# A mixer stage in another order: weight units, head statistics, convolution taps, roundings, low parts and a norm on TensorE, ScalarE and VectorE

## The chip, the cores and the metric

The kernel is one program on one core of a Trainium2 chip. The core has TensorE (PE, matmuls; PEld is its weight load), VectorE (DVE), ScalarE (ACT), GpSimd (POOL) and SyncE (SP), which here does nothing but issue DMAs. The metric is the device time of one execution in microseconds, lower is better; a kernel is judged by the median of its runs.

## The reference

Two transformer-like blocks of two layers each run on 256 tokens of 1024 channels in fp32. Every layer has a swiglu part, a mixer part and a swiglu part. The change touches the mixer of the first block, which runs twice (layer 0 and layer 1). Cut to its core:

```python
hn = _modulate(_rms_norm(h, norm_g[l, 1]), sh2, sc2)
z = hn @ w_in[l]                                   # 2564 columns
qa, ka = rms_norm per 32 channels of z             # dq, dk
o_a = differential_attention(qa, ka, va, lam)      # dv is the value
o_b = silu(layer_norm(conv31(a * sigmoid(g)) + b)) # ca, cg
u, v = split(gelu(z[..., GMLP0:FOX_Q0]))           # gu, gv
o_c = u * (W_s @ layer_norm(v) + bias)
log_f = log_sigmoid(z[..., FOX_F0:IN_COLS] + fb)   # f: four columns
o_d = forgetting_attention(rms_norm(q), rms_norm(k), v, log_f)   # fq, fk, fv
h = h + g2 * (concat(o_a, o_b, o_c, o_d) @ w_out[l])
```

`mod = silu(c) @ ada_w[l] + ada_b[l]` gives the shifts, scales and gates. Its 1024 x 3072 slice for the NEXT part is computed inside the present part, on VectorE.

## The kernel before

**Weight units.** All weights pass in units of 128x2048 fp32 (1 MB), unit k in slot k mod 3 of three buffers. SP loads a unit into `raw` (L375), ScalarE rounds it to fp32r, `whi` (`hi(L, k)`, L1117), VectorE subtracts that from it, `wlo` (`lo(L, k)`, L1648), and TensorE makes each product in three matmuls (L533 to L535), so that it needs `lo` of the unit and therefore `hi` and the load. In the mixer, units 0 to 10 are slices of `w_in` in the order fv, dv, gv, f, dq, dk, ca, cg, fq, fk, gu, and units 11 to 14 are `w_out`. I write z5 for TensorE's work on unit 5. f has four columns and is small. ScalarE copies the result of each unit out of PSUM (`copy(i)`, L1441); two PSUM banks take turns.

**Modulation tiles.** VectorE also multiplies 24 tiles of `ada_w` (128x1024, 0.5 MB each, L1775), `ada(m, q)`, written `tiles(first, last)`. There are two tile buffers.

**SP's queue.** SP is one queue in order. In the mixer it issues, for i = 0, 1, 2 ...: load of unit i, then tiles 2i-6 and 2i-5. Each has a wait of its own in that queue:

```python
sp.wait_ge(lo_done, L.unit(k, i) + 1)          # load: lo of unit k-3 is done
sp.wait_ge(adam_used, 24 * (m - 1) + q + 1)    # tile q: ada(q-2) is done
```

So the queue's order there is: load 6, tiles 6 and 7, load 7, tiles 8 and 9, load 8, tiles 10 and 11, load 9, and so on. Since tile 7 waits for ada(5), load 7 stands behind a wait for ada(5); load 8 behind one for ada(7), load 9 behind one for ada(9).

**The rest around the change.** On TensorE: `head_stat` (L784, mean squares of heads; the first needs the Square of dq and dk, L1468), `gmix` (L1026, needs the gmlp norm `gv`, L2133), `diff_scores` (L748), `taps` (L994, one 31-tap convolution diagonal each, from six buffers that POOL fills, L2294), `turn` (L767). On ScalarE: `rs` (L1283, L1284: Ln, then Exp, for 1/root), the forget gate's Abs, Exp and Ln (L1459 to L1461, each waits for VectorE's `fx`), softmax (L1295). On VectorE: the gelu and layer norm of gv (L2092 to L2133), the cumulative sum of the forget gates (L2142 to L2147, needs `fl` of ScalarE), `head_norm` (L1656 to L1659, L2099, needs `rs`), `conv_in` (L2166), `logits` (L1864 to L1879). Every engine goes through its own list in order and stops at the first wait that isn't met.

Of the kernel before, what the change touches and what calls it, by code (L numbers as in the profile page):

```python
# [5 lines left out]
ALU = mybir.AluOpType  # L6
# [34 lines left out]
def program(nc, x, c, ada_w, ada_b, norm_g, ffn1_w_in, ffn1_w_out, ffn2_w_in, ffn2_w_out, w_in, w_out,  # L41
# [5 lines left out]
    S = x.shape[1]  # L47
# [11 lines left out]
    with ExitStack() as ctx:  # L59
# [469 lines left out]
        def _(pe):  # L529
# [439 lines left out]
            def mix0(L, n, j, k0):  # L969
                l, m, at = L.l, n + 1, k0 + len(ZU1)  # L970

                def z(i):
                    unit_z(L, n, k0, i, ZU1[i][2])
# [4 lines left out]
                def diff_scores(c):  # L978
                    dq, dk = halves("dq"), halves("dk")
                    if c == 0:  # L980
                        pe.wait_ge(s["diffqk"], l + 1)
                    else:
                        pe.wait_ge(s["scores_read"], seq(L, ROUNDS, 1))
                    scores(L, st, dq, lambda r, w, ch: dk[r:r + w, ch, :],
                           lambda h: (64 * (h % 2) + 32 * c, h // 2), 32)
# [31 lines left out]
                z(3)  # L1017
                z(4)
                z(5)

                pe.wait_ge(s["gv"], l + 1)
                v = zt["gv"].rearrange("p (b e) -> p b e", b=2)
# [5 lines left out]
                ins.then_inc(s["gmix"], 1)  # L1028

                head_stat(L, 0, 0, blk32, sq8, [ps[:, 6, :], ps[:, 7, :]])  # L1030
                z(6)
                z(7)
                diff_scores(0)
                z(8)
                diff_scores(1)
                taps(0, 8)
                z(9)
                head_stat(L, 1, 1, blk64, sq8, [ps[:, 6, :], ps[:, 7, :]])
                taps(8, 16)
                z(10)  # L1040
                turn(L, 0, S0)
                taps(16, 24)
# [46 lines left out]
        def _(act):  # L1089
# [344 lines left out]
            def mix0(L, n, j, k0):  # L1434
                l, m = L.l, n + 1

                def copy(i, func=ACT.Copy):

                    used(L, k0 + i)
                    w = S if ZU1[i][2] == "F" else 2 * S  # L1440
                    act.activation(Z[:, i, 0:w], ps[:, i % 2, 0:w], func).then_inc(z_copied[0], 1)  # L1441

                hi(L, k0 + 2)
                copy(0)
                hi(L, k0 + 3)
                copy(1)
                hi(L, k0 + 4)
                copy(2)

                copied(L, zi["gv"])  # L1450
                act.activation(zt["cg"], zt["gv"], ACT.Square).then_inc(s["gu_sq"], 1)
                act.wait_ge(s["gu_t"], 2 * l + 1)
                act.activation(zt["cg"], zt["cg"], ACT.Sigmoid, scale=-GELU_B).then_inc(s["gu_e"], 1)

                hi(L, k0 + 5)
                copy(3)
                act.wait_ge(s["fx"], l + 1)
                f, w = zt["f"][0:4, 0:S], zt["f"][0:4, S:2 * S]
                st(act.activation(w, f, ACT.Abs))  # L1459
                st(act.activation(w, w, ACT.Exp, scale=-1.0))  # L1460
                act.activation(w, w, ACT.Ln, bias=ones_col[0:4, 0:1]).then_inc(s["fl"], 1)  # L1461

                hi(L, k0 + 6)
                copy(4)
                hi(L, k0 + 7)
                copy(5)
                copied(L, zi["dk"])
                act.activation(sq8h[0], Z[:, zi["dq"]:zi["dq"] + 2, :].rearrange("p a n -> p (a n)"),  # L1468
                               ACT.Square).then_inc(s["sq"], 1)
                rs(st, L.event(0), sq8h[1], stat2)  # L1470
                hi(L, k0 + 8)
                copy(6)
                hi(L, k0 + 9)
                act.wait_ge(s["gv"], l + 1)
                copy(7, ACT.Sigmoid)
                hi(L, k0 + 10)
                copy(8)
                softmax(L, 0, S0)
                hi(L, k0 + 11)
                copy(9)  # L1480
                copied(L, zi["fk"])
                act.activation(sq8h[0], Z[:, zi["fq"]:zi["fq"] + 2, :].rearrange("p a n -> p (a n)"),
                               ACT.Square).then_inc(s["sq"], 1)
                softmax(L, 1, S1)
                act.wait_ge(s["conv_in"], l + 1)
                rs(st, L.event(1), zca, stat2)
                hi(L, k0 + 12)
                copy(10)

                copied(L, zi["gu"])  # L1490
                act.wait_ge(s["scores"], seq(L, ROUNDS, 2))
                act.activation(zt["dq"], zt["gu"], ACT.Square).then_inc(s["gu_sq"], 1)
                turned_out(L, 0, PT1)
                act.wait_ge(s["gu_t"], 2 * l + 2)
                act.activation(zt["dq"], zt["dq"], ACT.Sigmoid, scale=-GELU_B).then_inc(s["gu_e"], 1)
                act.wait_ge(s["gu"], l + 1)
                act.activation(xo(4, 6), zt["gu"], ACT.Copy).then_inc(s["outh"], 1)

                act.wait_ge(s["pv"], seq(L, TURNS, 1))
                act.wait_ge(s["foxqk"], l + 1)  # L1500
                act.activation(u8[:, 1536:2048], ps[:, 7, :], ACT.Square).then_inc(s["sq"], 1)
                rs(st, L.event(2), sq8[:, 1536:2048], ps[:, 6, :])
                softmax(L, 2, S1)
                act.wait_ge(s["dout"], l + 1)
                act.activation(xo(0, 2), s0f[:, 1024:1536], ACT.Copy).then_inc(s["outh"], 1)

                act.wait_ge(diag_used, TAPS * (l + 1))
                for ch in range(2):
                    act.activation(zt["ca"][:, ch * S:ch * S + S], ps[:, PVB, ch * S:ch * S + S], ACT.Identity,
                                   bias=prm[:, CB + 2 * l + ch:CB + 2 * l + ch + 1]).then_inc(s["conv_done"], 1)  # L1510
                hi(L, k0 + 13)
                turned_out(L, 1, PT1)
                act.wait_ge(s["craw"], l + 1)
                act.activation(zt["cg"], zt["ca"], ACT.Square, scale=2.0).then_inc(s["sq"], 1)
                rs(st, L.event(3), nrm[:, 0, :], ps[:, 0, S:2 * S])
                act.wait_ge(s["pv"], seq(L, TURNS, 2))
                act.activation(xo(6, 8), ps[:, PVB, :], ACT.Copy).then_inc(s["outh"], 1)
                summed(m, 0)
                hi(L, k0 + 14)
                summed(m, 1)  # L1520
                act.wait_ge(s["cy"], 2 * l + 1)
                act.activation(zt["cg"], zt["ca"], ACT.Sigmoid).then_inc(s["cexp"], 1)
                act.wait_ge(s["cy"], 2 * l + 2)
                act.activation(xo(2, 4), zt["ca"], ACT.Copy).then_inc(s["outh"], 1)
                hi(L, k0 + 15)
                summed(m, 4)
                summed(m, 5)
# [12 lines left out]
        def _(dve):  # L1540
# [540 lines left out]
            def mix0(L, n, j, k0):  # L2081
# [26 lines left out]

                v = zt["gv"].rearrange("p (b e) -> p b e", b=2)
                gelu_in(1, zt["gv"], zt["cg"])  # L2110
                tiles(4, 5)
                dve.wait_ge(s["gu_e"], 2 * l + 1)
                st(tt(zt["gv"], zt["gv"], zt["cg"], ALU.mult))
                for b in range(2):
                    ins = dve.bn_stats(lnst[:, b, :], v[:, b, :])
                st(ins)
                dve.sem_inc(dve_waited, 1)
                for b in range(2):
                    ins = dve.bn_aggr(lnmv[:, b, :], lnst[:, b, :])
# [5 lines left out]
                for _ in range(3):  # L2125
                    st(tt(tmp, y, y, ALU.mult))
                    st(tt(tmp, tmp, half, ALU.mult))
                    st(stt(y, tmp, 1.5, y, ALU.add, ALU.mult))
                for b in range(2):
                    ins = ts(v[:, b, :], v[:, b, :], lnmv[:, b, 0:1], y[:, b:b + 1], ALU.subtract, ALU.mult)  # L2130
                st(ins)
                st(tt(v, v, ngb[:, 0, l:l + 1, :].to_broadcast([P, 2, 256]), ALU.mult))
                tt(v, v, ngb[:, 1, l:l + 1, :].to_broadcast([P, 2, 256]), ALU.add).then_inc(s["gv"], 1)  # L2133
                tiles(5, 6)
                lo(L, k0 + 5)

                copied(L, zi["f"])
                f, w = zt["f"][0:4, 0:S], zt["f"][0:4, S:2 * S]
                ts(f, f, fb[0:4, l:l + 1], None, ALU.add).then_inc(s["fx"], 1)
                tiles(6, 8)  # L2140
                dve.wait_ge(s["fl"], l + 1)
                st(stt(f, f, 0.0, w, ALU.min, ALU.subtract))  # L2142
                dve.tensor_tensor_scan(gcum[0:4, 0, 0:P], ones_row[0:4, :], f[:, 0:P], 0.0, ALU.mult, ALU.add)
# [1 line left out]
                st(dve.tensor_tensor_scan(gcum[0:4, 0, P:S], ones_row[0:4, :], f[:, P:S], gcum[0:4, 0, P - 1:P],  # L2145
                                          ALU.mult, ALU.add))
                ts(gcum[0:4, 1, :], gcum[0:4, 0, :], -1.0, None, ALU.mult).then_inc(s["foxcum"], 1)  # L2147
                lo(L, k0 + 6)
                tiles(8, 10)
                lo(L, k0 + 7)  # L2150

                dve.wait_ge(s["gmix"], l + 1)
                tg = zt["gv"].rearrange("p (c b t) -> p c b t", c=2, b=2)
# [1 line left out]
                for b in range(2):  # L2155
                    ins = tt(tg[:, :, b, :], mg[:, :, b, :], bsb[:, l, :, :], ALU.add)
                ins.then_inc(s["gmixed"], 1)
                tiles(10, 12)
                head_norm(0, sq8h[1], diffg, ("dq", "dk"), "diffqk")
                lo(L, k0 + 8)  # L2160
                tiles(12, 14)
                lo(L, k0 + 9)

                copied(L, zi["cg"])
                dve.memset(ypad[:, :, 0:CONVK - 1], 0.0)
                tt(ypad[:, :, CONVK - 1:], ca2, zt["cg"].rearrange("p (c t) -> p c t", c=2),  # L2166
                   ALU.mult).then_inc(s["conv_in"], 1)

                logits(L, st, 0, S0, amask, 32 ** -0.5)
                tiles(14, 16)  # L2170
                lo(L, k0 + 10)
# [171 lines left out]
```

## Time and profile before

| | |
|---|---|
| median of 3 runs (lowest, highest) | 2483.33 us (2475.29, 2487.5) |
| the profiled execution's own time | 2485.93 us |
| its span | 2484.1 us |
| PE, PEld, DVE, ACT busy | 92%, 77%, 65%, 45% |
| mean granted TensorE clock | 0.97 |
| DMA | 452.76 MB, 182 GB/s in the mean |

The span is that of all instructions; the time is 1.8 us more. A 92% busy PE bounds the kernel, and what can be won or lost is PE's idle time (and stretches at half clock). The first block's mixer runs from about 265 to 450 us (layer 0) and again from about 860 to 1045 us (layer 1).

### The profile page before, as it was taken

What the parts mean: (1) busy time and instruction counts of PE and PEld (TensorE: products, weight loads), DVE (VectorE), ACT (ScalarE), POOL (GpSimd) and SP (SyncE); (2) the same over time, 40 slices, a digit from 0 to 9 for tenths busy, and PEclk for the clock granted to TensorE, in tenths of its full rate; (3) what the DMA queues carried; (4) which work ended last, traced back from release to release, by engine and by line L of the source; (5) the groups of instructions that cost most, each with busy time, mean ns of one, the idle gap of its engine ahead of it and who ended that gap; (6) DMA issues with size and microseconds to landing.
All of it is one profiled execution on the core that took longest, in us unless ns stands there. A gap on an engine that the chain in (4) does not pass through costs nothing.

```text
span 2484.1 us, 31758 instructions
## 1 busy us (share of the span) xinstructions
PE 2297.6 (92%) x11778; PEld 1922.9 (77%) x11788; DVE 1604.2 (65%) x1886; ACT 1115.4 (45%) x1304; POOL 120.0 (5%) x176
## 2 busy tenths in 40 slices
PE   1999899899899989899989999989999998998998
PEld 0787777688688777678878889977877888997887
DVE  6686794676677677555565568675555556856555
ACT  1443463444444455344444456644444446564443
POOL 1000023000000004200000000000000000000000
PEclk9999998999999998899999999999999999999999
DMA  7787552587488564255555554345555555434653
GB/s 251 254 309 237 171 199 85 175 285 258 131 295 282 164 214 142 94 169 187 185 169 186 188 151 136 119 151 188 186 169 171 185 186 144 144 102 136 198 184 108
DMA packets 321123, 452.76 MB, mean 182 GB/s; under 512 B 32406, under 2 KB 269832, under 8 KB 320008
## 3 DMA queue, kind: packets, MB, share of 16 engines
q1 hardware_dynamic: 314160, 439.43, 54.1%
q0 software_dynamic: 2816, 9.51, 1.2%
q10 hardware_dynamic: 4056, 2.58, 0.4%
q8 instruction: 60, 0.98, 0.2%
q14 instruction: 31, 0.25, 0.0%
HBM read 450.43 MB, written 1.05 MB: 182 GB/s over the span
## 4 chain that ended last, share of the span: by engine, by line
PE 76%; DVE 13%; ACT 4%; issue 2%; POOL 1%; DMA 1%; ACTq 1%; DVEq 0%; SPq 0%
PE ps L540 18%; PE ps L541 18%; PE ps L542 18%; PE ps L533 3%; DVE wlo L1648 3%; PE ps L534 3%; PE ps L535 3%; PE ps L994 2%; PE ps L639 1%; POOL side L2294 1%; ACT whi L1117 1%; DMA arena<-in_ada_w_dram 1%; PE ps L748 1%; DVE arena L1775 1%; PE ps L589 1%
## 5 line engine op out<-in xcount | busy, mean ns | idle before, releaser
L1648 DVE TENSOR_TENSOR wlo<-raw,whi 128x2048 fp32r<-128x2048 f32 (+1 forms) x348 | 791.7, 2278 | 472.1 <-ACT whi L1117 472.1
L1117 ACT ACTIVATE whi<-raw 128x2048 fp32r<-128x2048 f32 x346 | 659.8, 1909 | 271.9 <-PE ps L542 235.6
L540 PE MATMUL ps<-whi,xl 128*128 128x512 f32 x1472 | 597.8, 406 | 22.9 <-DVE u L1792 22.9
L541 PE MATMUL ps<-wlo,xh 128*128 128x512 f32 x1472 | 579.1, 393 | 0.0
L542 PE MATMUL ps<-whi,xh 128*128 128x512 f32 x1472 | 578.4, 393 | 0.0
L540 PEld LDWEIGHTS ps<-whi,xl 128*128 128x128 f32 x1472 | 279.6, 190 | 86.4 <-DVE u L1792 26.3
L542 PEld LDWEIGHTS ps<-whi,xh 128*128 128x128 f32 x1472 | 279.6, 190 | 61.1
L541 PEld LDWEIGHTS ps<-wlo,xh 128*128 128x128 f32 x1472 | 279.8, 190 | 59.7 <-issue 4.8
L533 PE MATMUL ps<-xl,whi 128*128 128x256 f32 x864 | 254.0, 294 | 23.0 <-DVE wlo L1648 23.0
L540 PE MATMUL ps<-whi,hidl 128*128 128x512 f32 x640 | 252.2, 394 | 0.0
L542 PE MATMUL ps<-whi,hidh 128*128 128x512 f32 x640 | 249.2, 389 | 0.0
L541 PE MATMUL ps<-wlo,hidh 128*128 128x512 f32 x640 | 249.1, 389 | 0.0
L534 PE MATMUL ps<-xh,wlo 128*128 128x256 f32 x864 | 248.2, 287 | 0.0
L535 PE MATMUL ps<-xh,whi 128*128 128x256 f32 x864 | 247.9, 287 | 0.0
L1233 ACT ACTIVATE hidh<-ps 128x512 fp32r<-128x512 f32 x80 | 47.9, 599 | 319.6 <-PE ps L639 319.6
L533 PEld LDWEIGHTS ps<-xl,whi 128*128 128x128 f32 x864 | 169.8, 196 | 27.3 <-DVE wlo L1648 21.7
L534 PEld LDWEIGHTS ps<-xh,wlo 128*128 128x128 f32 x864 | 170.0, 197 | 1.1 <-issue 1.0
L535 PEld LDWEIGHTS ps<-xh,whi 128*128 128x128 f32 x864 | 169.6, 196 | 0.0
L1775 DVE SCALAR_TENSOR_TENSOR arena<-arena,condT 128x1024 f32<-128x1024 f32 x120 | 154.4, 1286 | 19.5 <-DMA arena<-in_ada_w_dram 17.8
L1229 ACT ACTIVATE sq<-ps 128x256 f32<-128x256 f32 x176 | 67.5, 384 | 219.4 <-PE ps L542 218.9
L1796 DVE TENSOR_TENSOR hidl<-ps,hidh 128x512 fp32r<-128x512 f32 x80 | 55.4, 692 | 160.6 <-ACT hidh L1233 160.6
L540 PEld LDWEIGHTS ps<-whi,hidl 128*128 128x128 f32 x640 | 120.2, 188 | 25.9 <-issue 1.4
(367 smaller groups left out, 2612.6 us busy)
## 6 DMA issues: line engine op xcount, KB each, us to landing
raw<-in_ffn_w_in_dram SPq DMA_DIRECT2D x176, 512.0 KB
arena<-in_ada_w_dram SPq DMA_DIRECT2D x128, 512.0 KB, 5.8
raw<-in_w_in_dram SPq DMA_DIRECT2D x54, 1024.0 KB
raw<-in_ffn_w_out_dram SPq DMA_DIRECT2D x44, 1024.0 KB
raw<-in_w_ffn_gate_dram SPq DMA_DIRECT2D x88, 512.0 KB
raw<-in_w_ffn_up_dram SPq DMA_DIRECT2D x88, 512.0 KB
raw<-in_w_ffn_down_dram SPq DMA_DIRECT2D x44, 1024.0 KB
raw<-in_w_out_dram SPq DMA_DIRECT2D x16, 1024.0 KB
```

Of the source, the lines that this page charges most:

```text
L533: pe.matmul(o, wh, al, start=start, stop=False, **kw)
L534: pe.matmul(o, wl, ah, start=False, stop=False, **kw)
L535: return pe.matmul(o, wh, ah, start=False, stop=stop, **kw)
L540: pe.matmul(o, al, wh, start=start, stop=False, **kw)
L541: pe.matmul(o, ah, wl, start=False, stop=False, **kw)
L542: return pe.matmul(o, ah, wh, start=False, stop=stop, **kw)
L994: pe.matmul(ps[:, PVB, ch * S:ch * S + S], diag[d % RING], ypad[:, ch, tap:tap + S], start=(tap == 0), stop=(tap == CONVK - 1)).then_inc(d ...
L1117: act.activation(whi[:, k % 3, :], raw[:, k % 3, :], ACT.Copy).then_inc(hi_done, 1)
L1229: act.activation(sig[:, a, :], ps[:, a, 0:256], ACT.Sigmoid).then_inc(sig_ready, 1)
L1648: tt(a[0], a[1], a[2].bitcast(F32), ALU.subtract).then_inc(lo_done, 1)
L1775: stt(seg, adam[:, at, :], scalar, seg, ALU.mult, ALU.add).then_inc(adam_used, 1)
L1796: tt(hidl[:, :, :].rearrange("p f t -> p (f t)"), ps[:, HT, :], hidh[:, :, :].bitcast(F32).rearrange("p f t -> p (f t)"), ALU.subtract).th ...
```

## The change

Only the order in which TensorE, ScalarE and VectorE go through their lists in `mix0` is changed, in the first third of it; SP's and POOL's lists stay as they are. On TensorE z6 moves ahead of `gmix`, z8 ahead of the first `diff_scores`, the first eight taps between the two `diff_scores`, and taps 8 to 16 ahead of the second `head_stat`. On ScalarE `hi` of units 5, 6 and 7 moves ahead of the forget gate's functions, and `rs` behind `hi` of units 8 and 9. On VectorE `lo` of units 5 to 9 moves earlier and the tiles later.

```diff
 # TensorE
+                z(6)
                 pe.wait_ge(s["gv"], l + 1)
...
                 head_stat(L, 0, 0, blk32, sq8, [ps[:, 6, :], ps[:, 7, :]])
-                z(6)
                 z(7)
+                z(8)
                 diff_scores(0)
-                z(8)
+                taps(0, 8)
                 diff_scores(1)
-                taps(0, 8)
                 z(9)
+                taps(8, 16)
                 head_stat(L, 1, 1, blk64, sq8, [ps[:, 6, :], ps[:, 7, :]])
-                taps(8, 16)
                 z(10)
 # ScalarE
                 act.activation(zt["cg"], zt["gv"], ACT.Square).then_inc(s["gu_sq"], 1)
+                hi(L, k0 + 5)
                 act.wait_ge(s["gu_t"], 2 * l + 1)
                 act.activation(zt["cg"], zt["cg"], ACT.Sigmoid, scale=-GELU_B).then_inc(s["gu_e"], 1)
-                hi(L, k0 + 5)
                 copy(3)
+                hi(L, k0 + 6)
+                copy(4)
+                hi(L, k0 + 7)
                 act.wait_ge(s["fx"], l + 1)
...
-                hi(L, k0 + 6)
-                copy(4)
-                hi(L, k0 + 7)
                 copy(5)
...
-                rs(st, L.event(0), sq8h[1], stat2)
                 hi(L, k0 + 8)
                 copy(6)
                 hi(L, k0 + 9)
+                rs(st, L.event(0), sq8h[1], stat2)
 # VectorE
                 gelu_in(1, zt["gv"], zt["cg"])
-                tiles(4, 5)
+                lo(L, k0 + 5)
...
+                copied(L, zi["f"])
+                ts(f, f, fb[0:4, l:l + 1], None, ALU.add).then_inc(s["fx"], 1)
...
+                lo(L, k0 + 6)
                 for b in range(2):
                     ins = ts(v[:, b, :], v[:, b, :], lnmv[:, b, 0:1], y[:, b:b + 1], ALU.subtract, ALU.mult)
...
-                tiles(5, 6)
-                lo(L, k0 + 5)
-                copied(L, zi["f"])
-                ts(f, f, fb[0:4, l:l + 1], None, ALU.add).then_inc(s["fx"], 1)
-                tiles(6, 8)
+                tiles(4, 6)
+                lo(L, k0 + 7)
                 dve.wait_ge(s["fl"], l + 1)
...
-                lo(L, k0 + 6)
-                tiles(8, 10)
-                lo(L, k0 + 7)
+                tiles(6, 8)
                 dve.wait_ge(s["gmix"], l + 1)
...
+                lo(L, k0 + 8)
+                tiles(8, 10)
+                lo(L, k0 + 9)
+                head_norm(0, sq8h[1], diffg, ("dq", "dk"), "diffqk")
                 tiles(10, 12)
-                head_norm(0, sq8h[1], diffg, ("dq", "dk"), "diffqk")
-                lo(L, k0 + 8)
-                tiles(12, 14)
-                lo(L, k0 + 9)
...
+                tiles(12, 14)
                 logits(L, st, 0, S0, amask, 32 ** -0.5)
```

VectorE's list before, in layer 0, from `lo` of unit 5 on. L1648 is a `lo`, here of units 5, 6 and 7; L1775 is a modulation tile, here 6 and 7, 8 and 9, then 10 and 11.

```order
 L1648 TENSOR_TENSOR wlo<-raw,whi 128x2048
 L2139 TENSOR_SCALAR arena<-arena,fb 4x256
 L1775 SCALAR_TENSOR_TENSOR arena<-arena,condT 128x1024 x2
 L2142 SCALAR_TENSOR_TENSOR arena<-arena 4x256
 L2143 SCALAR_TENSOR_TENSOR arena<-ones_row,arena 4x128
 L2145 SCALAR_TENSOR_TENSOR arena<-ones_row,arena 4x128
 L2147 TENSOR_SCALAR arena<-arena 4x256
 L1648 TENSOR_TENSOR wlo<-raw,whi 128x2048
 L1775 SCALAR_TENSOR_TENSOR arena<-arena,condT 128x1024 x2
 L1648 TENSOR_TENSOR wlo<-raw,whi 128x2048
 L2156 TENSOR_TENSOR arena<-ps,side 128x2x128 x2
 L1775 SCALAR_TENSOR_TENSOR arena<-arena,condT 128x1024 x2
```

The changed kernel's list, from the tiles 4 and 5 on. The L1648 rows are `lo` of units 7, 8 and 9, and the L1775 rows tiles 4 and 5, 6 and 7, 8 and 9.

```order
 L1775 SCALAR_TENSOR_TENSOR arena<-arena,condT 128x1024 x2
 L1648 TENSOR_TENSOR wlo<-raw,whi 128x2048
 L2141 SCALAR_TENSOR_TENSOR arena<-arena 4x256
 L2142 SCALAR_TENSOR_TENSOR arena<-ones_row,arena 4x128
 L2144 SCALAR_TENSOR_TENSOR arena<-ones_row,arena 4x128
 L2146 TENSOR_SCALAR arena<-arena 4x256
 L1775 SCALAR_TENSOR_TENSOR arena<-arena,condT 128x1024 x2
 L2153 TENSOR_TENSOR arena<-ps,side 128x2x128 x2
 L1648 TENSOR_TENSOR wlo<-raw,whi 128x2048
 L1775 SCALAR_TENSOR_TENSOR arena<-arena,condT 128x1024 x2
 L1648 TENSOR_TENSOR wlo<-raw,whi 128x2048
 L1656 TENSOR_TENSOR u<-sq 128x1024
```

Before, `lo` of unit 7 stood behind tile 9; now it stands directly behind tile 5, that of unit 8 behind tile 7, and that of unit 9 directly behind tile 9.

ScalarE's list, changed kernel, in the same place, with the semaphores that each waits for. L1117 are `hi` of units 5, 6, 7 and then 8 and 9; L1462 to L1464 are the forget gate's functions (L1459 to L1461 before).

```order
 L1117 ACTIVATE whi<-raw 128x2048 [waits unit_used,raw_loaded1]
 L1462 ACTIVATE arena<-arena 4x256 [waits fx]
 L1463 ACT_TABLE_LOAD
 L1463 ACTIVATE arena<-arena 4x256 [waits act_step]
 L1464 ACT_TABLE_LOAD
 L1464 ACTIVATE arena<-arena,ones_col 4x256 [waits act_step]
 L1441 ACTIVATE arena<-ps 128x512 [waits unit_used]
 L1468 ACTIVATE sq<-arena 128x1024 [waits z_copied0]
 L1117 ACTIVATE whi<-raw 128x2048 [waits unit_used,raw_loaded2]
 L1441 ACTIVATE arena<-ps 128x512 [waits unit_used]
 L1117 ACTIVATE whi<-raw 128x2048 [waits unit_used,raw_loaded0]
 L1283 ACTIVATE sq<-ps,epsc 128x1024 [waits ms_ready]
```

The first row is `hi` of unit 7, which was behind the forget gate's functions and now stands ahead of them, of `copy(5)` and of the Square (L1468); the last is `rs`, which was ahead of `hi` of unit 8 and now stands behind `hi` of unit 9.

## Rows read from the trace of the kernel before

**Rows 1.** TensorE's waits, 260 to 420 us: total, times, longest

```profile
PE ps L533 <- DVE wlo L1648: 7.0, 2, 6.1
PE ps L994 <- POOL side L2294: 5.0, 7, 1.4
...
PE ps L784 <- ACT sq L1482: 1.8, 1, 1.8
```

**Rows 2.** Windows: length, busy PE, PEld, DVE, ACT, POOL; PEclk, DMA share, GB/s

```profile
293.00:300.00 7.00, 6.02 (x48) 5.82 (x48) 6.35 (x20) 2.71 (x3) 0.00 (x0) 1.00 0.95 326
...
306.00:308.00 2.00, 1.97 (x9) 1.97 (x10) 1.90 (x3) 1.71 (x3) 0.00 (x0) 0.50 1.02 376
```

**Rows 3.** Timeline of TensorE: start, us, instruction, idle before and releaser

```profile
306.03 0.58 PE L533 MATMUL ps<-xl,whi 128*128 128x256 f32 x1 [6.06 <-DVE wlo L1648]
...
313.69 1.15 PE L1026 MATMUL ps<-arena 128*64 128x128 f32 x16
315.93 1.98 PE L784 MATMUL ps<-sq,blk 128*128 128x512 f32 x4 [1.09 <-ACT sq L1468]
317.35 0.68 PE L533 MATMUL ps<-xl,whi 128*128 128x256 f32 x1
...
346.76 0.47 PE L533 MATMUL ps<-xl,whi 128*128 128x256 f32 x1
...
365.65 1.47 PE L767 MATMUL ps<-ident,arena 128*128 128x128 f32 x12
```

**Rows 4.** SP's DMA issues in order of time (tiles L450, unit loads L375)

```profile
296.43 7.76 SPq L450 DMA_DIRECT2D arena<-in_ada_w_dram  x2
304.30 0.41 SPq L375 DMA_DIRECT2D raw<-in_w_in_dram  x1
...
317.47 0.41 SPq L375 DMA_DIRECT2D raw<-in_w_in_dram  x1
```

**Rows 5.** Timeline of VectorE

```profile
296.26 0.68 DVE L2113 TENSOR_TENSOR arena<-arena 128x512 f32<-128x512 f32 x1
...
302.50 1.28 DVE L1775 SCALAR_TENSOR_TENSOR arena<-arena,condT 128x1024 f32<-128x1024 f32 x1
...
310.26 0.41 DVE L2142 SCALAR_TENSOR_TENSOR arena<-arena 4x256 f32<-4x256 f32 x1 [1.45 <-ACT arena L1461]
...
312.06 2.29 DVE L1648 TENSOR_TENSOR wlo<-raw,whi 128x2048 fp32r<-128x2048 f32 x1
314.27 2.67 DVE L1775 SCALAR_TENSOR_TENSOR arena<-arena,condT 128x1024 f32<-128x1024 f32 x2
...
322.03 1.29 DVE L1775 SCALAR_TENSOR_TENSOR arena<-arena,condT 128x1024 f32<-128x1024 f32 x1 [1.03 <-DMA arena<-in_ada_w_dram]
323.23 1.22 DVE L1656 TENSOR_TENSOR u<-sq 128x1024 f32<-128x1024 f32 x1
...
329.07 2.28 DVE L1648 TENSOR_TENSOR wlo<-raw,whi 128x2048 fp32r<-128x2048 f32 x1
...
340.46 2.69 DVE L1775 SCALAR_TENSOR_TENSOR arena<-arena,condT 128x1024 f32<-128x1024 f32 x2
...
360.53 1.76 DVE L2184 TENSOR_TENSOR arena<-arena,u 128x1536 f32<-128x1536 f32 x1
```

**Rows 6.** Timeline of ScalarE

```profile
306.26 0.42 ACT L1459 ACTIVATE arena<-arena 4x256 f32<-4x256 f32 x1 [8.56 <-DVE arena L2139]
...
317.95 1.12 ACT L1283 ACTIVATE sq<-ps,epsc 128x1024 f32<-128x1024 f32 x1 [2.07 <-PE ps L784]
...
321.35 1.90 ACT L1117 ACTIVATE whi<-raw 128x2048 fp32r<-128x2048 f32 x1
...
325.27 1.92 ACT L1117 ACTIVATE whi<-raw 128x2048 fp32r<-128x2048 f32 x1 [0.97 <-DMA raw<-in_w_in_dram]
```

**Rows 7.** Layer 1: TensorE's longest wait; tiles 8 and 9; `hi` of unit 9

```profile
PE ps L533 <- DVE wlo L1648: 5.9, 1, 5.9
...
911.08 2.67 DVE L1775 SCALAR_TENSOR_TENSOR arena<-arena,condT 128x1024 f32<-128x1024 f32 x2
...
922.36 1.92 ACT L1117 ACTIVATE whi<-raw 128x2048 fp32r<-128x2048 f32 x1 [1.25 <-DMA raw<-in_w_in_dram]
```

More of the change, by code:

```diff
@@ L2116, in mix0 @@
                 st(ins)
+                copied(L, zi["f"])
+                f, w = zt["f"][0:4, 0:S], zt["f"][0:4, S:2 * S]
+                ts(f, f, fb[0:4, l:l + 1], None, ALU.add).then_inc(s["fx"], 1)
                 dve.sem_inc(dve_waited, 1)
@@ L2133, in mix0 @@
                 tt(v, v, ngb[:, 1, l:l + 1, :].to_broadcast([P, 2, 256]), ALU.add).then_inc(s["gv"], 1)
-                tiles(5, 6)
-                lo(L, k0 + 5)
-                copied(L, zi["f"])
-                f, w = zt["f"][0:4, 0:S], zt["f"][0:4, S:2 * S]
-                ts(f, f, fb[0:4, l:l + 1], None, ALU.add).then_inc(s["fx"], 1)
-                tiles(6, 8)
+                tiles(4, 6)
+                lo(L, k0 + 7)
                 dve.wait_ge(s["fl"], l + 1)
```

## The prediction

> **What bounds the kernel now.** I read the busy shares first, then TensorE's waits, its timeline, and those of the engines that feed it. TensorE is busy 92% of the span, so only its idle time and its slow stretches count. In the mixer of layer 0 its longest wait is for the low part of a weight unit: 7.0 us in two waits, of which the larger, 6.06, stands ahead of z5 [rows 1, 3]; layer 1 has the same, 5.9 us [rows 7]. The reader is to see what VectorE does meanwhile: from 296.26 on it goes through the norm of gv, then through tile 5 at 302.50 [rows 5], and only behind that comes `lo` of unit 5. After the gap the granted clock is at half, 0.50 [rows 2]: z5 took 313.69 - 306.03 = 7.66 us [rows 3], where the 48 matmuls of a unit at full clock take 6.02 [rows 2], so 1.64 more are lost. These 7.7 us a layer are what the new order can aim at. Otherwise TensorE waits there 1.09 us for the first head statistics [rows 3], 1.8 for the second, and 5.0 in all for POOL's diagonals [rows 1].
>
> **What else hangs on that order.** SP's list. Tiles 6 and 7 hold SP from 296.43 to 304.19, and load 7 goes out at 304.30 [rows 4]: half a microsecond after VectorE ended tile 5, at 302.50 + 1.28 = 303.78 [rows 5]. Load 9 goes out at 317.47 [rows 4], again half a microsecond after tile 9 ended, at 314.27 + 2.67 = 316.94 [rows 5]. What holds a load is the tile ahead of it in the queue, since `lo` of three units back was done long before. The trip from "tile 9 done on VectorE" to "unit 9 in SBUF" (the start of its `hi`, which waited for DMA) took 325.27 - 316.94 = 8.3 us [rows 5, 6], and in layer 1, from 913.75 to 922.36, 8.6 [rows 7]. It brings 2.1 MB, two tiles and a unit. Before, it is hidden: between tile 9 and `lo` of unit 9 VectorE has four more tiles, a head norm and two other `lo`.
>
> The Trainium skill (DMA: Bandwidth & Descriptors, "Anatomy of one DMA — SWDGE (gpsimd) path") says that a semaphore wait of a DMA is spent on the issuing sequencer, ahead of dispatch, and that the DMA engines only work off their queues. That speaks against this change, and the trace agrees with it.
>
> **The change, step by step** (layer 0, on the clock of before; a trip is taken as R = 8.0 us, a little under the two rows, because behind both a further tile was in the queue).
>
> Gain. z5 starts where z4 ends, 293.95 + 6.02 = 300.0, at full clock, with z6 right behind it until 312.0; before, z6 ended at 317.35 + 6.02 = 323.4 [rows 3]. TensorE is 11.4 us ahead, and `gmix` (1.15) ends at 313.2. The low parts are in time for it: `hi` of unit 5 can end at about 296, `lo` takes 2.2, so 298; of the norm (302.50 - 296.26 = 6.2 in all) some 4.1 stand ahead of `lo` of unit 6, and the bias of the gate 0.3, so it ends at 304.7.
>
> First trip. The last 2.1 of the norm and tiles 4 and 5 (2.6) bring VectorE to 309.4; it ended tile 5 at 303.78 before. Only then tile 7 and load 7 are issued, and unit 7 is there at 317.4. ScalarE has stood at `hi` of unit 7 since 302, and behind it in its list are the functions of the gate, the copy of z5 and the Square for the first `head_stat`. `hi` 1.9 gives 319.3, the functions 310.26 - 306.26 = 4.0 [rows 5, 6], copy 0.5, Square 1.1: 324.9. TensorE waits for that from 313.2, 11.7 us. Then `head_stat` 317.35 - 315.93 = 1.4 and a restart at half clock, 1.6: 327.9, and z7 until 333.9.
>
> Second trip. VectorE has `lo` of unit 7 by 321.6, waits for the gate until 323.3, cumulative sum 312.06 - 310.26 = 1.8 [rows 5], tiles 6 and 7 2.6: 327.7. Trip 335.7, `hi` 337.6, `lo` 339.8. TensorE waits 5.9 us; z8 with 1.6 of slow clock until 347.4.
>
> Third trip. Tiles 8 and 9 end at 342.4, trip 350.4, `hi` of unit 9 352.3. Only now comes `rs`: 321.35 - 317.95 = 3.4 [rows 6], 355.7, and `head_norm` 329.07 - 323.23 = 5.8 [rows 5], 361.5. The first `diff_scores` waits for it: 14.1 us of idle TensorE, then 3.2 and 1.6 of slow clock, 366.3, and eight taps, 5.1. VectorE does tiles 10 and 11 and `conv_in` until 364.8. Tile 13 is issued at 364.1 and lands some 5.1 later, as tile 11 did (issued after 316.94, used at 322.03 after a wait for DMA) [rows 5]; done at 370.5, the reading half of `logits` 1.9, 372.4. The second `diff_scores` runs until 375.6, where z9 starts; before it started at 346.76 [rows 3]: 28.8 us later.
>
> Given back. The 1.8 us wait at the second `head_stat` goes, since the taps cover it: 27.0. But `turn` waits for both softmaxes. Before, they took from 340.5 to 362.3, 21.8 [rows 5], of which ScalarE was held some 3 by the copy of z9, which isn't so now: from 374.3 to 393.1, against 365.65 [rows 3], 27.5 later. Behind that all follows as before; loads 10 and 11 are issued by 370 and are no limit.
>
> Sum: + 27.5 us a layer, two layers, + 55. The profiled execution took 2485.93, so 2540.9; the median of the runs is 2.6 under it, and I say 2538. The two moves of taps have no price of their own: POOL fills the same six buffers either way.
>
> **Bounds.** R at most 8.6 [rows 7], + 1.8 a layer. At least: 2.1 MB at 376 GB/s [rows 2] is 5.6 us, and the first tile of a pair leaves 1.3 us ahead of R's start, so 4.3 with nothing for start and completion, - 11 a layer. A restart costs 1.6 in the one case seen; after longer gaps 0 to 3 at each of three, - 5 to + 4 a layer.
>
> The Trainium skill's fit for one DMA (same page and section: about 2.0 us plus bytes at 436 GB/s) gives 6.8 us for 2.1 MB as an estimate, 5.5 from R's start; the sum by it would be 2523. This kernel's rows say 8.3 and 8.6, and I keep to them.
>
> **Rivals.**
> (a) Forecast: three exposed trips of 6.5 to 8.6 us with the work in series behind them, + 19 to + 33 a layer, 2521 to 2549. Chance 0.80.
> (b) Short trips: while VectorE stands still nothing follows in the queue, and a trip costs 5.6, the pure transfer at 376 GB/s; 3 x 2.4 = 7 less a layer, and with little lost clock 3 less again: + 17, 2517. Against it: tile 11 alone took 5.1. Chance 0.09.
> (c) Longer: the clock stays at half over much of 313 to 366 us, where TensorE works under half of the time; + 5 to 8 a layer more, 2548 to 2554. Chance 0.06.
> (d) Faster, the other side: SP doesn't hold load 7 behind tile 7. Then the early `lo` gains the 7.7 us and the 1.1 at the first `head_stat` a layer and nothing is given back, 2466. It decides if load 7 leaves before about 300. Against it: SP sat 7.76 us at tiles 6 and 7 with load 7 next in its list [rows 4]. Chance 0.03.
> (e) No change: the stalls are taken out of later waits. In the whole mixer TensorE waits little else than the 5.0 and 1.8 us of [rows 1]. Chance 0.02.
>
> Even trips of 0 us would not make it faster: 27.5 - 24 leaves 3.5 a layer, since `hi`, the functions of the gate, the Square, `rs` and `head_norm` now stand in series.
>
> **Numbers.** The likeliest is (a), 2538. The range takes in (a), most of (b) and (c): 2516 to 2556. A change within 0.5% (12 us) can't be told from none. Slower 0.95, within 0.02, faster 0.03.
>
> **What would show it.** Right: z5 and z6 run without a gap from 294 to 312; SP issues load 7 near 310, load 8 near 328, load 9 near 343, each half a microsecond behind the end of a tile; `hi` of units 7, 8 and 9 each wait for DMA; TensorE has gaps of about 12, 6 and 14 us ahead of the first L784, of z8 and of the first `diff_scores`; z9 starts near 376; the same again in layer 1. Wrong: load 7 issued before 305, or gaps that close because a trip takes under 5 us.

## The result, and the profile after

| | before | changed kernel |
|---|---|---|
| median of the runs | 2480.65 us (4 runs) | 2539.16 us (4 runs, 2535.13 to 2539.61) |
| span of the profiled execution | 2484.1 us | 2537.8 us |
| mean granted TensorE clock | 0.97 | 0.96 |

The ratio is 1.0231, 95% interval 1.0215 to 1.0248: 2.3% slower. Forecast were 2538 us and a range of 2516 to 2556. The span grew by 53.7 us. Three single executions, one each of the kernel before (5455 us), of experiment 1 (4585) and of experiment 2 (5814), lie far outside all others and are left out of the medians and ratios below.

TensorE's waits in the changed kernel, first layer 0, then layer 1. Each row has the total in us, how often, and the longest:

```profile
PE ps L748 <- DVE arena L2099: 14.9, 1, 14.9
PE ps L784 <- ACT sq L1468: 12.5, 1, 12.5
PE ps L533 <- DVE wlo L1648: 6.4, 2, 5.5
...
PE ps L748 <- DVE arena L2099: 14.7, 1, 14.7
PE ps L784 <- ACT sq L1468: 12.7, 1, 12.7
PE ps L533 <- DVE wlo L1648: 8.8, 2, 7.1
```

The 6.06 us ahead of z5 [rows 1, 3] are gone. In their place stand three gaps a layer: ahead of the first `head_stat` (L784), ahead of z8 (L533) and ahead of the first `diff_scores` (L748).

SP's issues of the changed kernel, layer 0: three times a pair of tiles (L450), then a unit load (L375). They answer to [rows 4]:

```profile
307.22 1.73 SPq L450 DMA_DIRECT2D arena<-in_ada_w_dram  x2
309.05 0.41 SPq L375 DMA_DIRECT2D raw<-in_w_in_dram  x1
325.77 1.72 SPq L450 DMA_DIRECT2D arena<-in_ada_w_dram  x2
327.60 0.41 SPq L375 DMA_DIRECT2D raw<-in_w_in_dram  x1
341.20 1.72 SPq L450 DMA_DIRECT2D arena<-in_ada_w_dram  x2
343.03 0.41 SPq L375 DMA_DIRECT2D raw<-in_w_in_dram  x1
```

VectorE, changed kernel, the same stretch: a pair of tiles (L1775), then the wait ahead of `lo` (L1648):

```profile
305.85 2.68 DVE L1775 SCALAR_TENSOR_TENSOR arena<-arena,condT 128x1024 f32<-128x1024 f32 x2
318.86 2.29 DVE L1648 TENSOR_TENSOR wlo<-raw,whi 128x2048 fp32r<-128x2048 f32 x1 [10.33 <-ACT whi L1117]
...
324.42 2.65 DVE L1775 SCALAR_TENSOR_TENSOR arena<-arena,condT 128x1024 f32<-128x1024 f32 x2
...
337.62 2.29 DVE L1648 TENSOR_TENSOR wlo<-raw,whi 128x2048 fp32r<-128x2048 f32 x1 [9.89 <-ACT whi L1117]
339.83 2.67 DVE L1775 SCALAR_TENSOR_TENSOR arena<-arena,condT 128x1024 f32<-128x1024 f32 x2
352.93 2.29 DVE L1648 TENSOR_TENSOR wlo<-raw,whi 128x2048 fp32r<-128x2048 f32 x1 [10.42 <-ACT whi L1117]
```

ScalarE, changed kernel: `hi` of units 7, 8 and 9, each after a wait for DMA:

```profile
316.92 1.91 ACT L1117 ACTIVATE whi<-raw 128x2048 fp32r<-128x2048 f32 x1 [15.74 <-DMA raw<-in_w_in_dram]
...
335.68 1.91 ACT L1117 ACTIVATE whi<-raw 128x2048 fp32r<-128x2048 f32 x1 [11.44 <-DMA raw<-in_w_in_dram]
...
350.98 1.91 ACT L1117 ACTIVATE whi<-raw 128x2048 fp32r<-128x2048 f32 x1 [12.91 <-DMA raw<-in_w_in_dram]
```

Read the three together. Tile 5 ends at 305.85 + 2.68 = 308.53, load 7 leaves half a microsecond later, unit 7 is used at 316.92: a trip of 8.4 us. The second runs from 327.07 to 335.68, 8.6, the third from 342.50 to 350.98, 8.5. Each time VectorE stands 10 us: the trip and `hi`. Layer 1 has the same picture, with trips of 8.7, 9.3 and 8.6 us.

TensorE, changed kernel: the first row answers to L784 of [rows 3]; the next are the scores and the eight taps between them, z9's first matmul, and `turn`:

```profile
324.30 3.78 PE L784 MATMUL ps<-sq,blk 128*128 128x512 f32 x4 [12.53 <-ACT sq L1468]
...
362.28 5.90 PE L748 MATMUL ps<-arena 32*128 32x128 f32 x16 [14.92 <-DVE arena L2099]
368.11 6.54 PE L994 MATMUL ps<-arena,side 128*128 128x256 f32 x16
374.57 3.60 PE L748 MATMUL ps<-arena 32*128 32x128 f32 x16
378.10 0.58 PE L533 MATMUL ps<-xl,whi 128*128 128x256 f32 x1
...
397.51 1.47 PE L767 MATMUL ps<-ident,arena 128*128 128x128 f32 x12
```

This trace runs 0.8 us ahead of that of before at z4, so `turn` is 397.51 - 365.65 + 0.8 = 32.7 us late [rows 3], and some 6 us of that are given back later in the layer.

### The profile page after: what moved, and what is told of

Read it like the earlier page. It is cut to its first block, busy times and chain, and to the rows that moved or that the text cites. A ratio compares the mean times of both kernels' runs of the same rounds, so it can differ in the third digit from the quotient of the medians.

```text
span 2537.8 us, 31772 instructions
## 1 busy us (share of the span) xinstructions
PE 2303.6 (91%) x11788; PEld 1927.7 (76%) x11788; DVE 1604.1 (63%) x1886; ACT 1114.4 (44%) x1304; POOL 117.1 (5%) x176
## 4 chain that ended last, share of the span: by engine, by line
PE 73%; DVE 14%; ACT 5%; DMA 3%; issue 2%; POOL 1%; ACTq 1%; SPq 0%; DVEq 0%
PE ps L540 18%; PE ps L542 18%; PE ps L541 18%; DVE wlo L1648 3%; PE ps L533 3%; PE ps L534 3%; PE ps L535 3%; DMA raw<-in_w_in_dram 3%; ACT whi L1117 2%; PE ps L639 1%; PE ps L994 1%; DVE arena L1775 1%; PE ps L748 1%; POOL side L2292 1%; PE ps L570 1%
## 5 line engine op out<-in xcount | busy, mean ns | idle before, releaser
L1648 DVE TENSOR_TENSOR wlo<-raw,whi 128x2048 fp32r<-128x2048 f32 (+1 forms) x348 | 791.7, 2278 | 533.6 <-ACT whi L1117 533.6
L1117 ACT ACTIVATE whi<-raw 128x2048 fp32r<-128x2048 f32 x346 | 660.0, 1910 | 393.4 <-PE ps L542 235.6
L533 PE MATMUL ps<-xl,whi 128*128 128x256 f32 x864 | 256.0, 296 | 22.8 <-DVE wlo L1648 22.8
L533 PEld LDWEIGHTS ps<-xl,whi 128*128 128x128 f32 x864 | 171.3, 198 | 28.4 <-DVE wlo L1648 21.5
L1775 DVE SCALAR_TENSOR_TENSOR arena<-arena,condT 128x1024 f32<-128x1024 f32 x120 | 154.2, 1285 | 23.5 <-DMA arena<-in_ada_w_dram 21.7
L541 PEld LDWEIGHTS ps<-wlo,hidh 128*128 128x128 f32 x640 | 120.2, 188 | 26.0 <-issue 1.4
```

The source lines that it names most:

```text
L533: pe.matmul(o, wh, al, start=start, stop=False, **kw)
L541: pe.matmul(o, ah, wl, start=False, stop=False, **kw)
L1117: act.activation(whi[:, k % 3, :], raw[:, k % 3, :], ACT.Copy).then_inc(hi_done, 1)
L1648: tt(a[0], a[1], a[2].bitcast(F32), ALU.subtract).then_inc(lo_done, 1)
L1775: stt(seg, adam[:, at, :], scalar, seg, ALU.mult, ALU.add).then_inc(adam_used, 1)
```

## The experiments

Two accounts were open. **The queue**: what bounds the stretch is a loop, tile on VectorE, SP, DMA, `hi` on ScalarE, `lo` on VectorE, and the change has put VectorE's `lo` directly behind the tiles that free the load. **The engines' own order**: TensorE's z6 and z8 ahead of small work, ScalarE's `hi` ahead of the gate's functions and `rs` behind `hi`, or VectorE's `head_norm` in series with the scores would cost time whatever SP does. Times are medians; "before" ran along each time, 2480.8 us with the first four and 2478.71 with the others. The ratios are to that "before"; the changed kernel has 1.0231 in the same sense.

**1. SP's loads 7 and 8 ahead of tiles 6 and 7** (the changed kernel, SP's list alone edited)

```diff
                                 load(L, k, whole(as8, k, cols8(w_in, l, col)))
-                            tiles(i)
+                            if i < 6:
+                                tiles(i)
+                            elif i > 7:
+                                tiles(i - 2)
...
-                            tiles(11 + g)
+                            tiles(9 + g)
+                        tiles(13)
+                        tiles(14)
```

> The changed kernel with one more edit, in SP's list of the first block's mixer alone: unit loads 7 and 8 go out ahead of tiles 6 and 7, and all later tiles follow two units later in the list (load 9, tiles 8 and 9, load 10, and so on). The engines' lists stay those of the changed kernel. Theory of the queue: what costs is the loop tile on VectorE, SP, DMA, hi, lo; with it cut, load 7 is issued near 293, hi of units 7, 8 and 9 hardly wait for DMA, VectorE's three waits of some 10 us ahead of L1648 go, and about 31 us a layer come back: 2477 us, between 2468 and 2488. Rival, the engines' own order (the functions of the gate behind hi, rs behind hi of unit 9, head_norm ahead of the scores in series): the gaps of TensorE at the first head_stat and the first diff_scores stay for the greater part, over 2510.

Measured 2477.14 us, ratio to before 0.9979 (0.9964 to 0.9994). SP's issues from load 6 on, of this kernel:

```profile
297.18 5.92 SPq L375 DMA_DIRECT2D raw<-in_w_in_dram  x3
312.49 1.75 SPq L450 DMA_DIRECT2D arena<-in_ada_w_dram  x2
```

TensorE's waits in it ahead of the scores (L753), the taps (L999) and `turn` (L772); the lines of this kernel stand 5 further down:

```profile
PE ps L753 <- DVE arena L2104: 4.2, 1, 4.2
PE ps L999 <- POOL side L2297: 2.5, 3, 1.2
PE ps L772 <- DVE arena L2187: 1.8, 1, 1.8
```

Loads 6, 7 and 8 now leave in one stretch from 297.18 (this trace is 5 us late at z4: 298.91 against 293.95), with tiles 6 and 7 behind them. The wait at the first `head_stat` is gone and that at the scores is 4.2 instead of 14.9. With the engines' lists untouched, all 62.0 us (2539.16 to 2477.14) come back. The loss was the loop; with this SP list the engines' order has no loss of its own. Its gain over before is 0.2%, some 2 us a layer. That is much less than the 7.7 us at z5: in this trace the scores and the eight taps behind the 4.2 us wait took 11.7 us at a mean granted clock of 0.56 (335.11 to 346.77). At full clock such scores take 3.2 and eight taps 3.6, so that wait and slow clock together cost about 9 us.

**2. `hi` of unit 7 back behind the Square** (changed kernel, ScalarE)

```diff
                 copy(4)
-                hi(L, k0 + 7)
                 act.wait_ge(s["fx"], l + 1)
...
                                ACT.Square).then_inc(s["sq"], 1)
+                hi(L, k0 + 7)
                 hi(L, k0 + 8)
```

> The changed kernel with hi of unit 7 moved back on ScalarE behind the functions of the forget gate, the copy of z5 and the Square. Theory of the queue: TensorE's 12.5 us wait at the first head_stat goes nearly whole, but the loop through VectorE, SP and DMA stays, so unit 7 lands when it did and a gap of about 7 us opens ahead of z7; VectorE gets the gate's values some 1.6 us earlier; all in all 1.8 us a layer less, 2536 us (2530 to 2540). Rival, TensorE's waits are what counts: 12.5 us a layer less, 2514.

Measured 2533.89 us (median of three; 2532.54 to 2540.51; ratio 1.0221, 1.0199 to 1.0243). TensorE's waits of this kernel, layer 0:

```profile
PE ps L533 <- DVE wlo L1648: 19.6, 3, 9.5
PE ps L748 <- DVE arena L2099: 14.9, 1, 14.9
```

The 12.5 us wait at L784 has vanished and stands again ahead of the weight units, 19.6 us instead of 6.4. The gain over the changed kernel is 5.3 us by the medians and about 2.5 by the ratios, for both layers together and inside the spread of these runs: the 25 us that the rival expected did not come. A wait that an engine shows can be only the place where a loop comes to the surface.

**3. Tiles 4 and 5 ahead of the norm** (changed kernel, VectorE)

```diff
                 lo(L, k0 + 5)
+                tiles(4, 6)
                 dve.wait_ge(s["gu_e"], 2 * l + 1)
...
-                tiles(4, 6)
                 lo(L, k0 + 7)
```

> The changed kernel with tiles 4 and 5 moved forward on VectorE to directly behind lo of unit 5, ahead of the norm, so that load 7 is issued near 300 and its trip lies under the norm; the trips of loads 8 and 9 stay as they are. Theory of the queue: the first of three trips is hidden, its wait on VectorE falls from 10.3 us to under 2, about 9 us a layer less: 2521 us (2513 to 2528), with the second and third wait of about 10 us unchanged. Rival: the second stall grows by what the first gives up (the order of the rest is too tight), 2535 to 2540.

Measured 2522.44 us (ratio 1.0170, 1.0143 to 1.0198). VectorE's and TensorE's waits of this kernel, layer 0:

```profile
DVE wlo L1648 <- ACT whi L1117: 22.0, 3, 10.6
...
PE ps L748 <- DVE arena L2099: 14.3, 1, 14.3
PE ps L533 <- DVE wlo L1648: 10.2, 2, 7.8
PE ps L784 <- ACT sq L1468: 1.6, 1, 1.6
```

Load 7 leaves at 302.09, its trip lies under the norm, and 16.7 us in two layers come back: one trip of three, 8.4 us a layer. VectorE's waits for `hi` in layer 0 are 22.0 us in place of 31.5, so two of 10 us are left. The second stall did not grow (the longest is 10.6 us, against 10.42).

**4. TensorE's list back as before** (changed kernel; z6 and z8 behind `head_stat` and the first scores, taps as before)

```diff
-                z(6)
                 pe.wait_ge(s["gv"], l + 1)
...
                 head_stat(L, 0, 0, blk32, sq8, [ps[:, 6, :], ps[:, 7, :]])
+                z(6)
                 z(7)
-                z(8)
                 diff_scores(0)
-                taps(0, 8)
+                z(8)
                 diff_scores(1)
+                taps(0, 8)
                 z(9)
-                taps(8, 16)
                 head_stat(L, 1, 1, blk64, sq8, [ps[:, 6, :], ps[:, 7, :]])
+                taps(8, 16)
```

> The changed kernel with TensorE's list as it was before the change (z6 behind the first head_stat, z8 between the scores, taps behind the second scores and behind the second head_stat), ScalarE and VectorE as changed. Theory of the queue: TensorE isn't what bounds this stretch, but z6 and z8 now stand behind the waits and not under them; 4 us a layer more, 2547 us (2540 to 2555). Rival, TensorE's order is part of the loss: at least 10 us a layer come back, under 2520.

Measured 2550.84 us (ratio 1.0298, 1.0278 to 1.0318), 12 more than the changed kernel. TensorE's waits of this kernel:

```profile
PE ps L748 <- DVE arena L2099: 22.1, 1, 22.1
PE ps L784 <- ACT sq L1468: 16.5, 1, 16.5
```

TensorE's part of the change softened the loss by 6 us a layer. It puts units under waits that come anyway: these two waits are 38.6 us here and 27.4 in the changed kernel.

**5. VectorE's part alone** (VectorE as changed, TensorE and ScalarE as before; the diff is the VectorE part of the one in "The change")

> Only VectorE's part of the change; TensorE's and ScalarE's lists as before. Theory of the queue: VectorE's list alone puts lo of units 7, 8 and 9 directly behind the tiles that free SP, so the whole loss is there, and more, since z6 and z8 stand behind the waits: 34 us a layer, 2549 us (2540 to 2560). Rival: most of the loss comes of ScalarE's list (hi ahead of the gate's functions, rs behind hi of unit 9), and this is under 2505.

Measured 2558.00 us (ratio 1.0318, 1.0296 to 1.0339). VectorE's list alone loses as much as all three parts and 19 us more.

**6. ScalarE's and TensorE's parts alone** (VectorE as before)

> Only ScalarE's and TensorE's parts of the change; VectorE's list as before. Theory of the queue: load 7 is issued near 304 as before, but hi of unit 7 now stands ahead of the gate's functions and of the Square, and rs behind hi of unit 9, so two of the trips are exposed through ScalarE's list though VectorE's isn't changed; 15 us a layer, 2511 us (2500 to 2522). Rival: without VectorE's part there is no loss, within 8 us of 2481.

Measured 2513.87 us (ratio 1.0140, 1.0110 to 1.0170). SP's load 7 in this kernel:

```profile
304.25 0.41 SPq L375 DMA_DIRECT2D raw<-in_w_in_dram  x1
```

The largest waits of TensorE and VectorE in it, and ScalarE's wait for the loads, which was 1.0 us before:

```profile
PE ps L533 <- DVE wlo L1648: 20.9, 4, 7.9
...
DVE arena L2142 <- ACT arena L1464: 7.2, 1, 7.2
...
ACT whi L1117 <- DMA raw<-in_w_in_dram: 18.4, 5, 7.8
```

Load 7 leaves as before (304.25), but `hi` stands ahead of the gate's functions on ScalarE and waits for it, and VectorE waits 7.2 us for the gate. So ScalarE's and TensorE's parts together cost 35 us (2513.87 - 2478.71). The rows point again to a wait for DMA in front of work that doesn't need it, but the two parts were not run apart, and this run alone doesn't show how much is whose. VectorE's part alone costs 79 (2558.00 - 2478.71), and all three 58 (2539.16 - 2480.65). They don't add up.

**7. The kernel before with the SP list of experiment 1**

> The kernel before, its engines' lists untouched, with SP's list of the first experiment. Theory of the queue: SP's list is only good for the VectorE list that it is written for. Here VectorE has tiles 8 and 9 directly behind lo of unit 6, and 10 and 11 directly behind lo of unit 7 and the gmix rows, while these tiles now stand behind loads that wait for just those lo: VectorE waits for DMA ahead of its tiles (not ahead of lo), and about 31 us a layer are lost, 2543 us (2515 to 2560). Rival, loads ahead are good by themselves and gave the gain of the first experiment: at most 2480.

Measured 2529.12 us (ratio 1.0205, 1.0183 to 1.0228). VectorE's longest wait of this kernel:

```profile
DVE arena L1780 <- DMA arena<-in_ada_w_dram: 29.5, 8, 6.6
```

SP's issues in it:

```profile
291.31 14.06 SPq L375 DMA_DIRECT2D raw<-in_w_in_dram  x3
305.48 0.97 SPq L450 DMA_DIRECT2D arena<-in_ada_w_dram  x2
```

Here the three loads take SP until 305.4, as load 8 waits for `lo` of unit 5, and the tiles stand behind: VectorE waits 29.5 us for tiles (L1780), where it waited 4.4 before. The loss is 50 us in place of the 62 expected. The list that saves 62 us under one VectorE order costs 50 under the other; loads ahead are not good by themselves.

**8. A version meant to beat both**: experiment 1 with head statistics and norm earlier

```diff
 # ScalarE
                 copy(6)
-                hi(L, k0 + 9)
                 rs(st, L.event(0), sq8h[1], stat2)
+                hi(L, k0 + 9)
 # VectorE
                 tiles(8, 10)
-                lo(L, k0 + 9)
                 head_norm(0, sq8h[1], diffg, ("dq", "dk"), "diffqk")
-                tiles(10, 12)
+                lo(L, k0 + 9)
+                tiles(10, 11)
...
-                tiles(12, 14)
+                tiles(11, 12)
                 logits(L, st, 0, S0, amask, 32 ** -0.5)
-                tiles(14, 16)
+                tiles(12, 14)
                 lo(L, k0 + 10)
+                tiles(14, 16)
```

> The kernel with loads 7 and 8 ahead (first experiment) and four more moves: on ScalarE rs for the first head statistics ahead of hi of unit 9; on VectorE head_norm ahead of lo of unit 9, tile 11 behind conv_in, tiles 12 and 13 behind logits(0), and lo of unit 10 ahead of tiles 14 and 15. Theory: with the queue cut, what bounds is VectorE's list between the first head_stat and the first softmax, seen as TensorE's 4.2 us wait ahead of the first diff_scores and its slow clock behind it, and VectorE's waits of 1.7 and 1.9 us for tiles 12 and 13; these go, about 5 us a layer: 2467 us (2460 to 2475). Rival: VectorE is full anyway and pushes the same wait to turn, 2475 to 2480.

Measured 2471.55 us (ratio to before 0.9970, 0.9958 to 0.9982), 0.3% under before. TensorE's waits, layer 0:

```profile
PE ps L999 <- POOL side L2298: 2.8, 4, 1.2
PE ps L772 <- DVE arena L2188: 1.9, 1, 1.9
PE ps L753 <- DVE arena L2104: 1.9, 1, 1.9
```

The wait at the scores fell from 4.2 to 1.9 us; that at `turn` (L772) stayed. The time is inside the expected range and short of its point, which was 10 us under experiment 1. By the medians it is 5.6 under it, but the "before" beside it was 2 us faster too, and by the ratios 2 us are left. The profile gives the direction, and the interval against before is clear of 1; between experiments 1 and 8 a gain is not shown.

## Why the prediction was right

**What bounds, and the gain.** As read: z5 and z6 run without a gap in the changed kernel, and the 6.06 us are gone. At that place the moves bring their 7.7 us a layer. As a gain of the kernel they are not shown: with the loss taken away, experiment 1 keeps some 2 us a layer, since a wait and a slow clock at the scores take the rest.

**SP's queue.** Load 7 was forecast near 310, 8 near 328, 9 near 343; measured 309.05, 327.60, 343.03. Experiment 1 shows by intervention that this hold is the whole loss. The prediction's side remark that 3.5 us a layer would be lost even with trips of 0 us, by work that now stands in series, concerns a case that no run made. Experiment 1, where loads 7 and 8 are not held by the tiles at all, has that same work in the same order and no loss.

**The trip.** Taken as 8.0 us, measured 8.4, 8.6 and 8.5 in layer 0: the rows' own 8.3 and 8.6 were right, and the discount for the tile behind them was not. Nothing was gained by an idle DMA, so the short-trip rival fell with it. By the Trainium skill's fit for one DMA (DMA: Bandwidth & Descriptors, "Anatomy of one DMA — SWDGE (gpsimd) path") the estimate was 5.5 us from the same start; the trace does not agree. The same section of the Trainium skill says that a semaphore wait is spent on the issuing sequencer ahead of dispatch. Experiments 1 and 7 agree: the order of SP's list alone moved the time by 62 and by 50 us.

**TensorE's idle time.** Forecast gaps of 11.7, 5.9 and 14.1 us; measured 12.5, 5.5 and 14.9.

**Two terms that were mis-sized and cancelled.** The step "a restart at half clock, 1.6" was too small. Behind the first gap `head_stat` and z7 lost 1.4 us each, but that stayed hidden, as z8 had to wait for its `lo` anyway; z8 lost 1.4; behind the third gap it showed. `turn` was forecast 27.5 us late and was 32.7. The windows of the changed kernel show why (PEclk is the third number from the end):

```profile
362.00:366.00 4.00, 3.67 (x11) 2.76 (x12) 3.31 (x5) 0.00 (x0) 0.00 (x0) 0.50 0.36 89
366.00:370.00 4.00, 4.00 (x12) 2.80 (x11) 1.34 (x2) 0.00 (x0) 0.37 (x1) 0.50 0.87 286
370.00:374.00 4.00, 4.00 (x11) 3.19 (x10) 3.97 (x5) 0.00 (x0) 2.59 (x5) 0.52 1.05 374
374.00:378.00 4.00, 3.94 (x19) 2.51 (x18) 3.26 (x4) 3.49 (x3) 0.81 (x3) 0.91 0.78 280
378.00:382.00 4.00, 4.00 (x19) 3.90 (x19) 2.77 (x3) 3.99 (x18) 0.00 (x0) 0.50 0.83 255
```

Behind the third gap the clock stays at half for 11 us, and it is at half again in z9, which took 8.6 us (378.10 to 386.74) and not 6.0. The scores took 5.9 for the forecast 4.8, the taps 6.5 for 5.1. So the path to `turn` was another than forecast: not the two softmaxes (TensorE has no wait at `turn` in layer 0), but TensorE's own list, busy without a gap from 378 to 398. In all `turn` came 5.2 us later than forecast: about 1.5 from the three trips (25.5 us in place of 24.0), the rest, near 4, from the clock. In layer 1 the scores took 5.9 us again, but the taps 5.1 and z9 its full-clock time; there `turn` did wait, 2.3 us, and was 29.9 us late, counted from z4 of that layer. The third rival named the mechanism, a longer time at half clock; it did occur, for the most part behind 366, where the rival's stretch ended, and the total that the rival gave did not.

The step "behind that all follows as before" was wrong in the other direction, by some 6 us in layer 0. The forget gate's small matmuls that follow the scores of the second attention ran at a higher clock than before, and so did the last taps. Windows of the same work, first in the kernel before:

```profile
377.81:388.01 10.20, 10.20 (x32) 8.22 (x33) 0.12 (x1) 1.19 (x1) 0.00 (x0) 0.52 0.36 139
403.60:417.20 13.60, 13.60 (x50) 11.35 (x51) 0.00 (x0) 2.48 (x3) 6.55 (x18) 0.80 0.03 9
```

And in the changed kernel:

```profile
408.68:416.68 8.00, 8.00 (x33) 6.51 (x33) 2.38 (x4) 2.40 (x3) 1.15 (x1) 0.67 0.79 260
432.20:443.20 11.00, 11.00 (x50) 9.48 (x51) 0.00 (x0) 2.50 (x3) 6.23 (x18) 1.00 0.04 13
```

These give back 2.2 and 2.6 us. One more comes from the taps behind `turn`, where a wait of 1.38 us for POOL's diagonal has gone and one of 0.59 for VectorE has come. Of the 32.7 us, 26.8 are left at the end of the mixer of layer 0. In layer 1 the mixer takes 28.6 us longer than before. From the sum of the two, the 0.8 us that this trace was ahead and about 1 us that comes back elsewhere lead to the 53.7 us of the span. So the forecast 27.5 a layer came out so near partly because the two errors cancelled, which is luck. Why the clock was higher there was not tried; it may be chance of phase, since both kernels do the same work in that place.

## What to carry to other kernels

Ahead of moving a transfer's consumer earlier, look at what stands ahead of that transfer in the issuing queue: here each load stood behind a tile that waits until VectorE has used the tile two before it. So `lo`, moved up directly behind the tile, put a whole round trip of 8.5 us on the path, three times a layer. Move the queue's list together with the engine's list, and never one alone: the same SP order gave 62 us with one VectorE order and took 50 with the other. A long wait of TensorE is not yet the cause: taking away one of 12.5 us in each layer gave 2 to 5 us in all, while hiding one trip that no row of TensorE names gave 8 us a layer.

## What the runs showed of the hardware

TensorE's granted clock can stay at half, and fall to half, while the engine is busy without a gap. In the changed kernel it was 0.50 from 362 to 373 us with TensorE busy 3.7 to 4.0 of every 4 us, on scores (32-row fp32 matmuls) and taps, behind a gap of 14.9 us. In layer 0 of the kernel before, the same scores and taps ran at 1.00 without a long gap ahead of them. But there the clock was at 0.52 in the mean from 377.81 to 388.01, with TensorE busy all of these 10.2 us on the forget gate's 4-row fp32 matmuls and no wait over 0.2 us in the 5 us ahead of them.

The gap ahead of the scores need not be long. In the profiled executions the first scores took 5.7 us behind a gap of 4.2 (experiment 1) and 5.9 behind 14.9 (the changed kernel), against 3.2 at full clock. Behind the gap of 12.5 us, with the plain weight unit z7 next, the clock was back at 1.00 by 331, some 7 us after work began. So in layer 0 a gap ahead of small matmuls cost more (2.7 us on the scores and 2.9 on the taps) than the 5.5 us gap ahead of weight unit z8 (1.4). These are single profiled executions, and no experiment varied the kind of work behind a gap by itself.
